# A recurrent mixer's second half, reordered into one pipeline on one core

## What is computed

```
# mixer_ab, h is (256, 1024); 8 heads of 64
S_t = S_{t-1} diag(w_t) - (S_{t-1} kk_t)(kk_t*a_t)^T + v_t k_t^T ;  y_t = S_t r_t
y_a = (group_norm(y) * lnx_g + lnx_b + sum(r*k*r_k) * v) * g
glu  = c_val * sigmoid(c_gate)
conv = causal depthwise conv over 31 tokens, 512 channels
y_b  = silu(layer_norm(conv))
out  = concat([y_a, y_b]) @ w_out
```

## Time and profile before

| | us |
|---|---|
| three runs | 2486.35, 2488.04, 2489.47 |
| median | 2488.04 |
| profiled execution | 2487.75 |
| its span | 2485.9 |
| PE busy | 2399.5 |
| DVE busy | 1458.1 |
| ACT busy | 1080.6 |
| POOL busy | 150.5 |

### The profile page before, as it was taken

One profiled execution on the slowest core, in us unless ns is written; L12 is line 12 of the kernel. 1 busy time (PEld: TensorE's weight loads), 2 busy tenths in 40 slices (PEclk: granted clock), 3 DMA queues, 4 the chain that ended last, 5 costly groups with the idle time before them and its releaser, 6 DMA issues.

```text
span 2485.9 us, 29666 instructions
## 1 busy us (share of the span) xinstructions
PE 2399.5 (97%) x11556; PEld 1982.3 (80%) x11556; DVE 1458.1 (59%) x1569; ACT 1080.6 (43%) x1335; POOL 150.5 (6%) x178
## 2 busy tenths in 40 slices
PE   6999998999999999999999999898999999999998
PEld 5888887888888888778887887697888888777887
DVE  3545766754645667675456456984545545645544
ACT  4434445343443444544444445353444444545442
POOL 0001000000000000000000002431000000200000
PEclk9999999999999999999999999998999999999999
DMA  6666444555655564455565565203556556343552
GB/s 218 206 207 214 171 136 150 203 171 186 204 180 186 199 205 170 136 187 179 186 218 170 190 226 175 72 1 133 178 191 199 179 191 200 115 139 119 191 190 92
DMA packets 281236, 426.57 MB, mean 172 GB/s; under 512 B 11747, under 2 KB 193635, under 8 KB 281136
## 3 DMA queue, kind: packets, MB, share of 16 engines
q1 hardware_dynamic: 272768, 399.67, 48.6%
q0 software_dynamic: 7520, 25.37, 3.3%
q10 hardware_dynamic: 864, 0.36, 0.1%
HBM read 422.49 MB, written 1.05 MB: 170 GB/s over the span
## 4 chain that ended last, share of the span: by engine, by line
PE 82%; DVE 12%; ACT 2%; issue 2%; POOL 2%; DMA 1%; SPq 1%; DVEq 0%; POOLq 0%; ACTq 0%
PE bank L1790 24%; PE bank L1792 24%; PE bank L1791 24%; DVE wl L1070 4%; PE bank L2200 2%; PE bank L1890 1%; PE bank L1837 1%; POOL rstd L445 1%; DVE stats L1105 1%; DVE arena L1536 1%; SPq L341 1%; DVE x L1114 1%; DVE y L1172 1%; PE bank L1992 1%; DVE y L1139 1%
## 5 line engine op out<-in xcount | busy, mean ns | idle before, releaser
L1070 DVE TENSOR_TENSOR wl<-wf,wh 128x2048 fp32r<-128x2048 f32 x355 | 809.4, 2293 | 416.2 <-ACT wh L614 415.8
L1790 PE MATMUL bank<-wh,xTh 128*128 128x512 f32 x2336 | 931.5, 399 | 34.9 <-DVE xTl L1084 26.9
L1792 PE MATMUL bank<-wh,xTl 128*128 128x512 f32 x2336 | 914.4, 391 | 0.0
L1791 PE MATMUL bank<-wl,xTh 128*128 128x512 f32 x2336 | 913.6, 391 | 0.0
L614 ACT ACTIVATE wh<-wf 128x2048 fp32r<-128x2048 f32 x355 | 673.4, 1915 | 248.9 <-PE bank L1792 244.4
L1790 PEld LDWEIGHTS bank<-wh,xTh 128*128 128x128 f32 x2336 | 442.8, 190 | 128.6 <-DVE xTl L1084 29.6
L1792 PEld LDWEIGHTS bank<-wh,xTl 128*128 128x128 f32 x2336 | 442.0, 189 | 94.2
L1791 PEld LDWEIGHTS bank<-wl,xTh 128*128 128x128 f32 x2336 | 443.1, 190 | 87.6 <-issue 0.7
L1790 PE MATMUL bank<-wh,hTh 128*128 128x512 f32 x704 | 276.9, 393 | 0.1
L1792 PE MATMUL bank<-wh,hTl 128*128 128x512 f32 x704 | 274.5, 390 | 0.0
L1791 PE MATMUL bank<-wl,hTh 128*128 128x512 f32 x704 | 274.0, 389 | 0.0
(11 more groups left out here) (317 smaller groups left out, 1554.8 us busy)
## 6 DMA issues: line engine op xcount, KB each, us to landing
wf<-in_ffn_w SPq DMA_DIRECT2D x160, 512.0 KB, 4.8
wf<-in_w_in SPq DMA_DIRECT2D x52, 1024.0 KB, 5.4
wf<-in_ffn_w SPq DMA_DIRECT2D x44, 1024.0 KB, 5.2
wf<-in_ffn_w_down SPq DMA_DIRECT2D x44, 1024.0 KB, 5.1
wf<-in_ffn_w_gate SPq DMA_DIRECT2D x80, 512.0 KB, 4.0
wf<-in_ffn_w_up SPq DMA_DIRECT2D x80, 512.0 KB, 4.9
wf<-in_w_branch SPq DMA_DIRECT2D x16, 1024.0 KB, 5.2
wf<-in_c_w_in SPq DMA_DIRECT2D x14, 1024.0 KB, 5.9
```

The lines of the kernel that those rows point to most:

```text
L1070: dve.tensor_tensor(wl[s], wf[s], wh[s].bitcast(f32), ALU.subtract).then_inc(SEM[f"lo{s}"], 1)
L1790: pe.matmul(o, lh, rh, start=start, stop=False)
L1791: pe.matmul(o, lh, rl, start=False, stop=False)
L1792: return pe.matmul(o, ll, rh, start=False, stop=stop)
```

## The change

It puts the 24 steps of group and round in one pipeline: PE makes Z products of step i, then the merge of step i - 2, then, from i = 5 to 16, one Gram product of the keys or of beta (a "fill"). All four channel tiles of the convolution are now DVE's: 31 taps of four instructions. ACT's scaled copies and POOL's additions for tile 3 are gone. The masks of the 12 key and beta Grams move behind the taps of their step. The mixed values and their shift DMA come later, `prep(3)` and one weight unit of PE change places with turned rows, and parts of w and of the outputs that don't need u are made inside the pipeline. After it, ACT does the SiLU before it copies u of block 1, the convolution's half of the projection input is turned and split first, the state's first terms are accumulated early, and the projection runs by parts: its first halves use the convolution. SP loads two weight slots of the next SwiGLU earlier. The core of the diff, with cuts:

```diff
-    gram_bank = (1, 3, 0, 2)
+    start_bank, z_bank, fill_bank = (1, 3, 4, 5), (1, 3), (0, 2)
+    FILLS = [("key", u) for u in range(4)] + [("beta", g) for g in range(2)] + [("key", u) for u in range(4, 8)] + [("beta", g) for g in (2, 3)]
+    FIRST_FILL = 3
...
# POOL
-        shift(kp, kq, "prev1_ld")
...
         for g in range(4):
             pool.wait_ge(SEM["n_ready"], c.next("n_ready"))
-            pool.tensor_tensor(DT_t[g], N_t[g], four(pair_t), ALU.mult).then_inc(SEM["dt_ready"], 1)
+            pool.tensor_tensor(DT_t[g], N_t[g], four(pair_t), ALU.mult).then_inc(SEM["dt0_ready"], 1)
+        shift(kp, kq, "prev1_ld")
...
-            pool.tensor_tensor(conv_o[:, 3, :], conv_o[:, 3, :], tap_s[:, n % 4, :], ALU.add).then_inc(SEM["tap"], 1)
...
# ACT
+        for i in range(24):
+            if i < 20:
+                copied(D_t, i, 4, "d_mm", "d_ready")
+            copied(DT_t, i, 6, "dt_mm", "dt_ready")
+            if i == 17:
+                taken(w_s, 0, 0, "w_mm", "w_ready")
+        act.wait_ge(SEM["rk_made"], c.next("rk_made"))
+        taken(u_s, 0, 4, "u_mm", "u_ready")
+        taken(w_s, 1, 2, "w_mm", "w_ready")
...
-        y_squares(0)
         for b in range(TB):
             silu_conv(b)
+        taken(u_s, 1, 4, "u_mm", "u_ready")
+        y_squares(0)
+        out_x(0, 1, 6)
+        out_x(1, 1, 7)
         y_squares(1)
+        out_x(0, 0, 4)
+        out_x(1, 0, 5)
         c.count("gen1", 3)
         c.count("gen0", 3)
-        for b in range(TB):
-            take_x(b)
         prep(4, 2)
         prep(5, 2)
         out_of_mixer(RMS)
...
# DVE
         def tap(j):
-            for ct in range(3):
-                dve.wait_ge(SEM["dve"], c.so_far("dve") - 2)
+            for ct in range(4):
+                dve.wait_ge(SEM["dve"], c.so_far("dve") - 3)
...
+        j = 0
+        for i in range(24):
+            masked(Z_t[i % 4], z_bank[i % 2], merge_m[i // 4 + 1], "z_mm", "zp_ready")
+            if i == 8:
+                dve.wait_ge(SEM["rk_made"], c.next("rk_made"))
+                dve.tensor_reduce(bonus, r_t.rearrange("p b (h n) -> p (b h) n", n=HD), X, ALU.add).then_inc(SEM["bonus_done"], 1)
+            for _ in range(2 if i % 2 and i > 8 else 1):
+                if j < CONV:
+                    tap(j)
+                    j += 1
+            if 0 <= i - 2 - FIRST_FILL < len(FILLS):
+                take_gram(i - 2 - FIRST_FILL)
...
+        centred(0)
+        out_x(0, 1, 6)
+        out_x(1, 1, 7)
         spread(0)
+        centred(1)
+        dve.wait_ge(SEM["post_made"], c.next("post_made"))
         gated_y(0)
-        centred(1)
         spread(1)
+        out_x(0, 0, 4)
         gated_y(1)
-        for b in range(TB):
-            take_x(b)
+        out_x(1, 0, 5)
...
# PE
+        for i in range(24):
+            z_products(i)
+            if i == 2:
+                pe.wait_ge(SEM["rows_ready"], c.next("rows_ready", 2))
+            if i > 1:
+                merge_products(i - 2)
+            if 0 <= i - 2 - FIRST_FILL < len(FILLS):
+                fill(i - 2 - FIRST_FILL)
+            if i == 18:
+                pe.wait_ge(SEM["gram_made"], c.next("gram_made", 2))
+                pe.wait_ge(SEM["v_in"], c.next("v_in"))
+                key_values(0, 0, 0, True, True).then_inc(SEM["w_mm"], 1)
+            if i == 20:
+                key_values(1, 2, 0, True, False)
+            if i == 22:
+                pe.wait_ge(SEM["w_ready"], c.so_far("w_ready") + 1)
+                key_values(0, 0, 1, True, False)
+        pe.wait_ge(SEM["d_ready"], c.next("d_ready", 20))
+        state_of(kappa, rv_t, True, False)
+        merge_products(22)
...
+        solved(0, 4)
+        merge_products(23)
+        pe.wait_ge(SEM["u_ready"], c.next("u_ready"))
+        state_of(beta, u_s, False, True).then_inc(SEM["s_mm"], 1)
+        updates_out(0, 0)
...
+        solved(1, 4)
         pe.wait_ge(SEM["u_ready"], c.next("u_ready"))
+        updates_out(1, 3)
...
+        for b in range(TB):
+            pe.wait_ge(SEM["yb_ready"], c.next("yb_ready"))
+            turn_half(y_conv[:, b, :], 6 + b)
+        pe.wait_ge(SEM["ya_ready"], c.next("ya_ready"))
+        turn_half(y_rwkv[:, 0, :], 4)
+        x_in()
+        part_unit(1, 1, 0, 0, True, False)
+        part_unit(2, 1, 0, 1, True, False)
+        x_in()
+        x_in()
+        part_unit(0, 0, 0, 0, False, True)
+        part_unit(3, 0, 0, 1, False, True).then_inc(SEM["half"], 1)
+        part_unit(1, 1, 1, 2, True, False)
+        pe.wait_ge(SEM["yc_ready"], c.next("yc_ready", TB))
+        pe.wait_ge(SEM["ya_ready"], c.next("ya_ready"))
+        turn_half(y_rwkv[:, 1, :], 5)
+        part_unit(2, 1, 1, 3, True, False)
+        x_in()
+        part_unit(0, 0, 1, 2, False, True)
+        turn(0, y, "x_ready")
+        part_unit(3, 0, 1, 3, False, True)
```

More of the change, by code:

```diff
@@ L906, in taken @@
             act.activation(dst[:, b, :], bank[bk][:, :], ACT.Copy).then_inc(SEM[to], 1)
-        for g in range(4):
-            take_rows(g, ROW_A)
-        prep(1)
[L911 to L933, removed]
+        for g in (0, 2):
+            take_rows(g, ROW_A, 4 + g)
+        prep(3)
+        for g in (1, 3):
+            take_rows(g, ROW_A, 4 + g)
+        for g in range(2):
+            take_rows(g, ROW_R, 6 + g)
+        prep(1)
+        for g in range(2, 4):
+            take_rows(g, ROW_R, 4 + g)
+        for i in range(24):
[7 more added lines that the diff above has]
+        taken(w_s, 1, 2, "w_mm", "w_ready")
         def silu_conv(b):
@@ L1550, in _ @@
             c.count("gram_ready", 2)
+        c.count("gen0")
+        unmixed(rv_t, mu_v, 0, 1)
+        for g in range(4):
+            masked(D_t[g], start_bank[g], pair_m, "turned", "d0_ready")
         mixed_in(rv_t, kp, "prev1_ld").then_inc(SEM["v_in"], 1)
-        for g in range(4):
-            masked(D_t[g], gram_bank[g], pair_m, "turned", "d_ready")
+        low(1)
         dve.wait_ge(SEM["v_in"], c.next("v_in"))
         dve.wait_ge(SEM["cw_ready"], c.next("cw_ready"))
-        for u in range(4):
-            key_grams(u)
@@ L1558, in _ @@
[L1558 to L1565, removed]
-        dve.wait_ge(SEM["lo1"], c.so_far("lo1"))
[L1567 to L1574, removed]
@@ L1575, in _, with take_gram @@
-        while j < CONV:
-            tap(j)
-            j += 1
+        dve.wait_ge(SEM["lo1"], c.so_far("lo1"))
+        def take_gram(f):
+            kind, n = FILLS[f]
+            dve.wait_ge(SEM["gram_mm"], c.next("gram_mm"))
+            o = bank[fill_bank[f % 2]][:, :]
+            if kind == "key":
+                dve.tensor_tensor(k_grams[n // 2][:, 2 * (n % 2):2 * (n % 2) + 2, :, :],
+                                  o.rearrange("p (a w t) -> p a w t", a=2, w=2),
+                                  gram_m.rearrange("p (a w) t -> p a w t", a=1).broadcast_to([P, 2, 2, P]), ALU.mult)\
+                   .then_inc(SEM["gram_made"], 1)
+            else:
+                dve.tensor_tensor(b_grams[n], o.rearrange("p (a t) -> p a t", a=4), four(gram_m[:, 1, :]), ALU.mult)\
+                   .then_inc(SEM["gram_made"], 1)
@@ L1578, in _ @@
+        assert j == CONV
         dve.wait_ge(SEM["dve"], c.so_far("dve"))
@@ new lines, in key_values, with state_in @@
+        def key_values(b, bk, w, start, stop, heads_=range(RH)):
+            for h in heads_:
+                ins = pe.matmul(bank[bk][:, h * HD:(h + 1) * HD], k_grams[2 * b + h % 2][:, h // 2, w, :], tokens(rv_t, b, h),
+                                start=start and h == 0, stop=stop and h == RH - 1)
+            return ins
+        def state_in(bk, w, stop):
+            for q in range(4):
+                ins = pe.matmul(bank[bk][:, q * P:(q + 1) * P], rows_T[1][:, q, w, :], state[:, q, :], start=False,
+                                stop=stop and q == 3)
+            return ins
@@ L2287, in _, with turn_half, part_unit @@
-        second_exit(lambda b, k: (y_rwkv if k < 4 else y_conv)[:, b, (k % 4) * P:(k % 4 + 1) * P], "ya_ready")
+        updates_out(1, 3)
+        def turn_half(src, bk):
+            for q in range(4):
+                ins = pe.transpose(bank[bk][:, q * P:(q + 1) * P], src[:, q * P:(q + 1) * P], ident[:, :])
+            ins.then_inc(SEM["tr"], 1)
+        def part_unit(s, h, b, bk, start, stop):
+            if b == 0:
+                pe.wait_ge(SEM[f"lo{s}"], c.next(f"lo{s}"))
+            t = slice(b * P, (b + 1) * P)
+            for q in range(4):
+                k = 4 * h + q
+                r = slice(q * HALF, (q + 1) * HALF)
+                ins = three(bank[bk][:, :], xTh[:, k, t], xTl[:, k, t], wh[s][:, r], wl[s][:, r], start and q == 0, stop and q == 3)
+            if b:
+                ins.then_inc(SEM[f"used{s}"], 1)
+            return ins
```

236 lines of the change are left out of this document (100 added, 136 removed).

## The result

The changed kernel takes 2499.66 us (median of five runs, 2496.82 to 2501.68), against 2488.04 before: a ratio of 1.0043, 95% interval 1.003 to 1.0055, so 11.6 us slower. The profiled execution took 2501.68, the longest of the five; its span is 2499.9, 14.0 more than before's. Of these, 0.8 is there before the change begins to act: DVE's shifted addition that starts at 1570.22 in the earlier trace rows starts at 1571.03.

What follows compares the result with a forecast made beforehand. PE is busy 97% of the span; only the mixer, 1570 to 1737 us, matters. Next SwiGLU at 1747.7 instead of 1737.3, +10.4, plus 2.8 for the clock: +13.2, so 2501.0 us; own range 2495 to 2507, 8-in-10 range 2484 to 2509.

Steps and rivals of the forecast that it cites:

- Up to the first mask: Part 1, mixed values to first Z mask: despite the later shift DMA, the mask starts at 1598.4, 4.9 us earlier.
- The 24 steps: Part 2, first to last Z mask: PE slower up to step 8, then DVE; last mask at 1678.9, 7 us later.
- With a fill 0.74 more: In the steps: a fill adds 0.74 us to PE's 2.7 per step, priced from four key Grams in 2.96.
- From there DVE is the slower one: From the bonus sum at 1621.7: DVE sets the pace for 50.8 us, plus 7.9 lost to POOL.
- Rival (b): In the steps: the exclusion of POOL and DVE costs nothing, taking off 7.9, to 2493.1 us; chance 0.12.
- Rival (d): In the steps: DVE-bound pauses drop the clock, PE at half speed bounds some six steps; 15 more, 2516; chance 0.08.
- exclusive lock: POOL's products beside DVE's taps: shared ports held for whole instructions; 7.9 us lost, or 9.5 by full exclusion.
- The chain: Part 3, last mask to first projection unit: late mask and u copy behind SiLU eat the gain; unit at about 1711.8.
- half of 5.6: PE pause before the state: a clock fall would add 5.6 us; half of it, 2.8, was taken.
- The exit: Part 4, projection to next SwiGLU: ACT's square queued late, x_ready 17.5 us after `half`, at 1742.2; SwiGLU at 1747.7.
- Rival (a): At the exit: it costs nothing, as the square isn't held or x_ready is late anyway; 2492.0 us; chance 0.15.
- (c): Exit and POOL's products both cost nothing, and the clock stays: 2481.3 us, faster; chance 0.10.

Runs made afterwards that it cites:

- e3: Changed kernel with the fills made in pairs on both row halves and two banks, at every second step: 2498.74 us, ratio 1.0044, first to last mask 83.8.
- e4: Changed kernel without POOL's products behind the bonus sum: 2494.38 us, ratio 1.0021, first to last mask 79.9.
- e5: Changed kernel without the 30 taps of channel tile 3 behind the first: 2497.01 us, ratio 1.0033, first to last mask 80.2.
- e10: Kernel before, with POOL's products behind the bonus sum moved behind its tap additions: 2482.47 us, ratio 0.9976, first to last mask 58.7.
- e2: Changed kernel with ACT's u copy of block 1 ahead of the SiLU: 2496.53 us, ratio 1.0032, chain 31.0.
- e7: Changed kernel with the edits of e1 and e2 and the bonus sum at step 2 instead of 8: 2488.35 us, ratio 0.9995, chain 27.7.
- e8: Changed kernel with the edits of e1 and e2, paired fills, and POOL's products held until the convolution's last tap: 2477.72 us, ratio 0.9962.
- e9: As e8 but without the paired fills: 2486.64 us, ratio 0.9991, first to last mask 79.9.
- second trace: The changed kernel run again, with nothing edited: 2498.02 us, ratio 1.0038, chain 31.6.
- e1: Changed kernel with ACT's square of block 0 ahead of the turned half and weight copies, DVE's norm ahead of their remainders: 2488.13 us, ratio 1.0002.

## Why the prediction was right, and where it wasn't

**Up to the first mask: right.** The shift DMA's wait, the addition beside POOL and the start of the first mask (1598.4 forecast, 1598.05 less 0.8 measured) follow the sum to 1.2 us.

**The 24 steps: the sum is near, the reading of it was wrong.** "With a fill 0.74 more" is the mis-sized term. The row it came from, four key Grams in 2.96, makes two on one row half and then two on the other without anything between; four lone fills would take 4 x 1.06 = 4.2. That products on the two halves overlap is shown by e3; that this is all of the difference isn't. A lone key fill costs 1.06 and a lone beta fill 1.09. A step with a fill is 3.93, not 3.44. Three fills lie ahead of step 8's mask, so that mask and the bonus sum came 1.1 to 1.2 later than forecast, the 0.8 taken off. From there DVE's sum held: 50.8 plus what POOL takes was to be 58.7; it was 58.1 (1623.66 to the end of the last tap, 1681.72), of which 6.7 went to POOL (5.33 - 1.66 and 6.25 - 3.25) instead of 7.9.

But "From there DVE is the slower one" is true only with POOL's products in. From the end of the bonus sum to the start of the last mask (1623.66 to 1679.45) are 55.8 us. DVE pauses for 0.4 of them and loses 6.7 to POOL, so its own work is 48.7. PE waits for 1.5, so its own work is 54.3. With POOL's share the two are about 1 us apart; without it PE is 5.6 longer. Two steps with fills cost PE 7.86 and DVE 7.15. DVE's row without a pause was not a proof that it alone bound: it was working off the backlog that it had from POOL's time, while PE set the pace. The chain of waits of the changed kernel has it:

```profile
1623.66 5.25 DVE arena L1526 x4
1630.11 6.17 DVE arena L1526 x8
1638.06 2.88 PE bank L2200 x24
1641.99 2.88 PE bank L2200 x24
1645.92 2.88 PE bank L2200 x24
```

DVE binds for two steps beside POOL, then PE, to the end. e4 and e5 show what hung on this: by my sum DVE would have given back 6.7 and, up to PE's own time, most of 11.9, and the steps gave 1.8 and 1.6. In this the near sum is luck: without POOL's share it would have been 7.9 lower, and the steps, by e4, 1.8. The steps' 81.4 us can be added up on PE: 58.7 for the steps without POOL's products (e10), 12 lone fills 12.8, three products for w and outputs 5.2, 12 x (3.93 - 2.69 - 1.06) = 2.2 around the fills, the one wait 1.5, together 80.4. Before, PE's steps stood beside a loss of 9.3 to POOL (68.0 - 58.7, e10). Rival (b), that POOL's products cost nothing, is nearer the truth for the steps than I gave it, by the mechanism it names: without the products PE is the slower one from step 9 on, by the lone fills, and of 6.7 only 1.8 came through. It doesn't give that rival's time, because what it takes off the sum PE's own fills put back. Rival (d), PE at half speed in the steps, falls: behind its cold start PE's 24 records take 2.94 in every step of the changed kernel with a fill.

The Trainium skill's exclusive lock ("SBUF — State Buffer", "Who interferes with whom") had been given the whole of the products' time. They run from 1623.73 to 1633.62, 9.9 us, and the taps lost 6.7 in that time; the masks, which read PSUM, kept their 0.68. That agrees with a shared port, but not with an exclusion for the whole time: the loss is 3.2 short of the products' 9.9. DVE's two masks in this time are 1.2 of the 3.2; in the other 2.0 it got on with taps.

**The chain: right in its order, two terms off.** The u copy behind the SiLU cost 3.9, shown by e2, e7, e8 and e9. The table load, which I put on the path at 1.28, was hidden: it ran at 1694.40, ahead of the wait for DVE's statistics, and the SiLU followed that wait. With the held clock the chain is 31.6 where I had 32.9: the 1.28. The drain that the Trainium skill adds ("ScalarE: Activation LUTs", "What ACT_TABLE_LOAD costs", about 1.38 us) can't be read there, as ACT waited anyway; in the kernel before, where it didn't wait, there is none: the load began at 1697.87 and took 1.28, and the ACTIVATE began at 1699.17. The fallen clock costs 3.3, not 5.6; that half of 5.6 came near it is chance. In the second trace the clock held, and it cost nothing.

**The exit: right in mechanism and size.** x_ready was forecast for 1742.2 + 2.8 = 1745.0 and came at 1743.94 + 1.28 = 1745.2; PE stood for 8.5 (9 forecast) and its next unit ran cold. e1 took the queue order away and gave 9.9. Rival (a) falls, and (c) with it. (Among the chances, "Faster 0.12" is called "most of c", which has only 0.10.)

**Open:** why the clock fell behind the 1.18 us pause in one execution and not in another of the same kernel, and how often it does in timed runs; why e2's timed gain is below its 3.9; and 1.8 of the 3.3 us between e8 and e9 late in the program.

## What to carry to other kernels

Price a lone piece of work from a row in which it ran alone: a price per piece taken from a row of many can hold an overlap that the change takes away. Before an engine without pauses is called the bound, sum its neighbour over the same steps and look at the chain of waits; where the two are close (here 7.86 and 7.15 us for two steps), taking from one gives little and taking from both gives more than the sum (1.8 and -2.0 alone, 6.7 together). And look at what stands ahead of the first link of the next stage in each engine's list: a square behind two weight copies cost 9.9 us, nearly as much as the whole change lost, and a block of GpSimd work on a path where VectorE was needed cost 7 us of the kernel before.

## What the runs showed of the hardware

Two sets of f32 products on 64 rows each, on the two row halves and into two banks, take the time of one: 1.13 us for 4 records and 1.13 for 8. GpSimd's products stretch VectorE's taps from 1.66 to 5.33 and leave its masks from PSUM at 0.68. In the changed kernel a table load didn't wait for its ACTIVATE's input: it ended at 1695.68, and the ACTIVATE began at 1700.87, behind a wait of 5.19 for VectorE. And a granted clock isn't settled by a kernel's order alone: behind one and the same pause of 1.18 us it was 0.54 in one execution and 1.00 in another.
